# Four norms of a two-block network applied late: unscaled rows turned in halves inside neighbouring products

## The reference

```
# first block
h = rms_norm(x, norm_mix_g);  proj = h @ w_in            # 7 parts of 1024 columns
merged = sigmoid(g_a) * sgu(u, v) + sigmoid(g_b) * attention(q, k, v)
x = x + merged @ w_out
h = rms_norm(x, norm_ffn_g);  x = x + square(relu(h @ w_ff1)) @ w_ff2
gate = sigmoid(rms_norm(x, norm_ple_g) @ w_ple_gate);  x = x + gate * (p @ w_ple_proj)
x = rms_norm(x, norm_final_g)
# second block
h = rmsnorm(x, norm_mix);  z, xbc, dt, q, k, v = split(h @ w_in_2)
x = x + concat(ssd(conv(xbc), dt) gated by z, windowed attention(q, k, v)) @ w_out_2
h = rmsnorm(x, norm_ffn);  router: best group of 8, its 2 best of 8 experts
x = x + sum of gate * expert(h)                          # 64 experts, three matrices of 1024x512 each
out = rmsnorm(x, norm_final)
rms_norm(x, g) = x * rsqrt(mean(x * x) + 1e-6) * g
```

## Time and profile before

| | us |
|---|---|
| median of three runs | 1657.46 |
| lowest and highest | 1656.88 and 1661.55 |
| profiled execution, its own time | 1659.11 |
| its span, first to last instruction | 1657.3 |
| mean granted TensorE clock | 0.958 of full |
| busy in the span: PE / DVE / ACT / POOL | 1506.3 / 574.6 / 452.0 / 27.7 |

### The profile page before, as it was taken

One profiled execution on the slowest core, in us unless ns is written; L12 is line 12 of the kernel. 1 busy time (PEld: TensorE's weight loads), 2 busy tenths in 40 slices (PEclk: granted clock), 3 DMA queues, 4 the chain that ended last, 5 costly groups with the idle time before them and its releaser, 6 DMA issues.

```text
span 1657.3 us, 20152 instructions
## 1 busy us (share of the span) xinstructions
PE 1506.3 (91%) x7956; PEld 944.9 (57%) x7958; DVE 574.6 (35%) x926; ACT 452.0 (27%) x720; POOL 27.7 (2%) x36
## 2 busy tenths in 40 slices
PE   7999978999979987879999898889889889999996
PEld 5897868988759977763343343434334333444342
DVE  5745656654464897631111011111101101111112
ACT  5435645533444554421111011111101111111111
POOL 1000000000000000120000000000000000000000
PEclk9999989999989997979999999999999999999998
DMA  8563343455334332577999999999999999999993
GB/s 295 167 235 109 120 152 135 173 203 183 122 116 139 103 102 72 194 300 332 422 406 429 429 428 428 429 429 428 429 429 427 429 429 384 408 425 415 418 397 138
DMA packets 80269, 489.21 MB, mean 295 GB/s; under 512 B 6423, under 2 KB 8595, under 8 KB 56788
## 3 DMA queue, kind: packets, MB, share of 16 engines
q1 hardware_dynamic: 79028, 484.17, 72.4%
q0 software_dynamic: 1184, 4.26, 0.8%
HBM read 506.20 MB, written 1.08 MB: 306 GB/s over the span
## 4 chain that ended last, share of the span: by engine, by line
PE 61%; DMA 15%; DVE 8%; issue 2%; ACT 1%; SPq 1%; DVEq 0%; ACTq 0%
PE bank L1156 23%; PE bank L818 20%; DMA slots<-in_w_up_dram 15%; PE bank L1192 8%; PE bank L1126 4%; PE bank L1136 2%; DVE w_split L1292 1%; DVE h_lo L1282 1%; DVE areas L1542 1%; DVE xeT L1726 1%; PE bank L801 1%; SPq L394 1%; PE bank L1075 1%; PE bank L1104 0%; PE bank L1065 0%
## 5 line engine op out<-in xcount | busy, mean ns | idle before, releaser
L1156 PE MATMUL bank<-slots,xeT 128*64 128x512 f32 x1536 | 356.4, 620 | 48.0 <-DMA slots<-in_w_up_dram 47.9
L1156 PEld LDWEIGHTS bank<-slots,xeT 128*64 128x64 f32 x1536 | 118.9, 143 | 280.4 <-issue 280.4
L1292 DVE TENSOR_TENSOR w_split<-raw,w_split 128x2048 fp32r<-128x2048 f32 (+2 forms) x98 | 209.1, 2168 | 75.4 <-ACT w_split L543 75.4
L1192 PE MATMUL bank<-slots,heT 128*64 128x512 f32 x1024 | 226.8, 595 | 7.5 <-ACT heT L747 7.5
L818 PE MATMUL bank<-w_split,h_hi 128*128 128x512 f32 (+1 forms) x688 | 213.8, 393 | 8.4 <-DVE h_lo L1282 3.3
L818 PE MATMUL bank<-h_hi,w_split 128*128 128x256 f32 x1120 | 206.9, 285 | 0.3 <-DVE h_lo L1282 0.3
L543 ACT ACTIVATE w_split<-raw 128x2048 fp32r<-128x2048 f32 (+2 forms) x98 | 173.6, 1817 | 62.3 <-PE bank L818 56.7
L818 PEld LDWEIGHTS bank<-h_hi,w_split 128*128 128x128 f32 x1120 | 176.7, 193 | 2.2 <-issue 0.8
L1735 DVE TENSOR_TENSOR h_e<-bank,h_e 128x512 f32<-128x512 f32 x32 | 22.1, 692 | 433.2 <-PE bank L1156 433.2
L818 PE MATMUL bank<-h_lo,w_split 128*128 128x256 f32 x560 | 159.0, 284 | 0.0
L1192 PEld LDWEIGHTS bank<-slots,heT 128*64 128x64 f32 x1024 | 70.7, 137 | 144.9 <-issue 133.5
(11 more groups left out here) (295 smaller groups left out, 1390.5 us busy)
## 6 DMA issues: line engine op xcount, KB each, us to landing
slots<-in_w_up_dram SPq DMA_DIRECT2D x64, 2048.0 KB, 18.9
slots<-in_w_down_dram SPq DMA_DIRECT2D x64, 2048.0 KB, 15.2
areas<-in_w_gate_dram SPq DMA_DIRECT2D x32, 2048.0 KB, 14.2
slots<-in_w_gate_dram SPq DMA_DIRECT2D x32, 2048.0 KB, 21.3
raw<-in_w_in_dram SPq DMA_DIRECT2D x42, 1024.0 KB, 6.1
raw<-in_w_ff_dram SPq DMA_DIRECT2D x32, 1024.0 KB, 5.2
raw<-in_w_out_dram SPq DMA_DIRECT2D x12, 1024.0 KB, 5.0
raw<-in_w_ple_gate_dram SPq DMA_DIRECT2D x4, 1024.0 KB, 5.6
```

What stands on the lines that cost most here:

```text
L1156: last = mm(bank[SLOTS * e:SLOTS * e + SLOTS, :], xeT[:, k, odd, SLOTS * e:SLOTS * e + SLOTS], expert_panel(w, e, odd)[:, k, :], start=(k ...
L1192: last = mm(banks[half][SLOTS * e:SLOTS * e + SLOTS, :], heT[:, c, SLOTS * e:SLOTS * e + SLOTS], expert_panel("down", e, odd)[:, c, 512 * ...
L1292: last = tt(lo, source, hi, ALU.subtract)
```

## The change

At the four later norms x itself is turned, not a scaled copy. The first half of its columns (places 0 and 1 of `turn`, k tiles 0 to 3) is turned in the middle of the last product before the norm, into banks that are free (`turn_bank`), the second half behind that product. The factor 1/rms is computed from x beside the products and multiplied in later. For ff1 the square of it goes into the addition of the ff2 result. For pg it is the scale of the sigmoid. For the second block it goes into z and v (scale along rows), into the scores of the attention (rows), and by a row laid out along the tokens (`scale_row`, two matmuls against the identity) into k, dt and xbc, of which GpSimd scales the half that ScalarE empties. For the router it goes into the logits and into t_all. The panel pp moves before ff2 6, its product is kept in SBUF (p_proj), and GpSimd makes xg. norm_final_g comes a second time, as columns, by one more small load, so that the two gains are multiplied once.

```diff
-          + [("ff1", j) for j in range(8)] + [("ff2", j) for j in range(8)]
-          + [("pp", 0), ("pg", 0), ("pg", 1)]
+          + [("ff1", j) for j in range(8)] + [("ff2", j) for j in range(6)]
+          + [("pp", 0), ("ff2", 6), ("ff2", 7), ("pg", 0), ("pg", 1)]
...
+        def turn_bank(t, b):
+            if t in (T_FFN, T_MIX2):
+                return banks[pair_of(AT["wo" if t == T_FFN else "pg", b // 2]) + b % 2]
+            if t == T_PLE:
+                return banks[2 - pair_of(AT["pg", 0]) + b % 2]
+            return banks[b]
...
+                sp.dma_start(final_rows, norm_final_g.rearrange("(c p) -> c p", p=P)).then_inc(rows_loaded, 16)
```

GpSimd:

```diff
+            for half in range(2):
+                at = slice(512 * half, 512 * half + 512)
+                pool.wait_ge(x_ready, X_MLP + 2 * half + 2)
...
+                nc.gpsimd.tensor_tensor(xg[:, :, at], x[:, :, at], final_g[:, at].unsqueeze(1).to_broadcast([P, MT, 512]),
+                                        ALU.mult).then_inc(xg_ready, 1)
...
+            pool.wait_ge(row_ready, 1)
+            for j in range(3):
+                pool.wait_ge(emptied_a, emptied("a", AT["xbc", j]))
+                part = xraw[:, 4 * j:4 * j + 2, TAPS - 1:]
+                nc.gpsimd.tensor_tensor(part, part, scale_row.unsqueeze(1).to_broadcast([P, 2, S]), ALU.mult).then_inc(xbc_scaled, 1)
...
+            for half in range(2):
+                pool.wait_ge(x_ready, X_OUT1 + 2 * half + 2)
+                for m in range(MT):
...
+                    nc.gpsimd.tensor_tensor(to, row, gain, ALU.mult).then_inc(t_made, 1)
```

ScalarE, around ff1 and pg:

```diff
-            split_panel(AT["ff1", 0])
-            norm_x(T_FFN)
-            turn(T_FFN)
-            split_panel(AT["ff1", 1])
+            split(2 * AT["ff1", 0])
+            turn(T_FFN, (0, 1))
+            split(2 * AT["ff1", 0] + 1)
+            turn(T_FFN, (2, 3))
+            split(2 * AT["ff1", 1])
+            norm_x(emptied_d, emptied("d", AT["wo", 1]), xn)
+            split(2 * AT["ff1", 1] + 1)
...
+            for half in range(2):
+                for m in range(MT):
+                    act_(p_proj[:, m, 512 * half:512 * half + 512], banks[2 * half + m][:, :], ACT.Copy).then_inc(p_kept, 1)
+            split_panel(AT["ff2", 7])
+            split(2 * AT["pg", 0])
+            turn(T_PLE, (0, 1))
+            split(2 * AT["pg", 0] + 1)
+            turn(T_PLE, (2, 3))
+            split(2 * AT["pg", 1])
+            norm_x(x_ready, X_MLP, rows_area(3))
+            split(2 * AT["pg", 1] + 1)
```

ScalarE, the rows of h for the experts:

```diff
+            act.wait_ge(rstd_ready, norms[0])
+            for m in range(MT):
+                act.wait_ge(t_made, 3 + m)
+                link(act_(t_all[:, m, :], t_all[:, m, :], ACT.Copy, scale=stats[:, 8 + m:9 + m]))
                 act_(t_hi[:, m, :], t_all[:, m, :], ACT.Copy).then_inc(t_rounded, 1)
```

TensorE before ff1 (the other three joins are alike):

```diff
-            for j in range(2):
-                whole("wo", j, T_MERGED if j == 0 else None)
-
-            normed_turn(T_FFN, AT["wo", 1])
+            whole("wo", 0, T_MERGED)
+            quarter("wo", 1, 0)
+            quarter("wo", 1, 1)
+            banks_empty(AT["wo", 0])
+            turn(T_FFN, (0, 1))
+            quarter("wo", 1, 2)
+            quarter("wo", 1, 3)
+            hT_ready(T_FFN, 3)
+            part("ff1", 0, 0, (0, 1))
+            banks_empty(AT["wo", 1])
+            turn(T_FFN, (2, 3))
+            part("ff1", 0, 0, (2, 3))
+            hT_ready(T_FFN)
+            part("ff1", 0, 1, range(4))
```

TensorE in ff2 7, between its halves, and in pg 0:

```diff
+                    if j == 7 and k == 4:
+                        pe.wait_ge(p_kept, 4)
+                        pe.wait_ge(x_ready, 2)
+                        turn(T_PLE, (0, 1))
...
+            hT_ready(T_PLE, 3)
+            quarter("pg", 0, 0)
             pe.wait_ge(x_ready, X_MLP)
+            turn(T_PLE, (2, 3))
```

TensorE before q2: places 0 and 1 are turned after two quarters of pg 1, 2 and 3 after `part("q2", 0, 0, (0, 1))`; then the rest of q2 0, the product for dt, and:

```diff
+            pe.wait_ge(rstd_ready, 5)
+            for m in range(MT):
+                last = mm(banks[5][:, P * m:P * m + P], mix_scale[:, m:m + 1].to_broadcast([P, P]), ident[:, :], start=True, stop=True)
+            last.then_inc(row_made, 1)
```

TensorE before the router:

```diff
+            project_out(1, False, True, (0, 1))
+            pe.wait_ge(x_ready, X_OUT1 + 2)
+            turn(T_FFN2, (0, 1))
+            project_out(1, False, True, (2, 3))
...
+            route(0)
+            pe.wait_ge(x_ready, X_MIX2)
+            turn(T_FFN2, (2, 3))
+            route(1).then_inc(routed, 1)
```

VectorE, the ff2 result and the gate:

```diff
+                    stt(part, banks[4 + 2 * m + half][:, :], ffn_scale[:, m:m + 1], part, ALU.mult, ALU.add).then_inc(x_ready, 1)
...
+            def add_ple(half):
...
+                for m in range(MT):
+                    dve.wait_ge(emptied_a, emptied("a", AT["pg", half]) - 1 + m)
+                    link(tt(gate_rows[:, m, at], gate_rows[:, m, at], p_proj[:, m, at], ALU.mult))
+                    tt(x[:, m, at], x[:, m, at], gate_rows[:, m, at], ALU.add).then_inc(x_ready, 1)
...
+            add_ple(0)
+            split(2 * AT["q2", 0])
+            turn(T_MIX2, (0, 1))
+            split(2 * AT["q2", 0] + 1)
+            add_ple(1)
+            turn(T_MIX2, (2, 3))
+            split(2 * AT["q2", 1])
```

VectorE, second attention, convolution and router:

```diff
-                tt(soft[:, b, 0:S], bank[:, 0:S], mask, ALU.add)
+                    stt(soft[:, b, 0:S], bank[:, 0:S], mix_scale[:, 1:2], mask, ALU.mult, ALU.add)
+                    stt(soft[:, b, S:384], bank[:, S:384], mix_scale[:, 0:1], own, ALU.mult, ALU.add).then_inc(scores_taken, 1)
...
-                dve.wait_ge(emptied_a, emptied("a", AT["xbc", j]))
+                dve.wait_ge(xbc_scaled, j + 1)
...
+            for m in range(MT):
+                last = ts(logits[:, m, :], banks[m][:, 0:72], stats[:, 8 + m:9 + m], None, ALU.mult)
```

More of the change, by code:

```diff
@@ L724, in _ @@
             split_panel(AT["wo2", 1])
-            norm_x(T_FFN2)
-            turn(T_FFN2)
+            load_roots()
+            for half in range(2):
+                turn(T_FFN2, (2 * half + 1,))
+                for m in range(MT):
+                    part = slice(512 * half, 512 * half + 512)
+                    last = act_(rows_area(2)[:, m, part], x[:, m, part], ACT.Square,
+                                accum_out=stats[:, 2 * half + m:2 * half + m + 1])
+            last.then_inc(squares, 1)
+            norm(T_FFN2, MT)
+            act.wait_ge(rstd_ready, norms[0])
             for m in range(MT):
-                act.wait_ge(t_made, m + 1)
+                act.wait_ge(t_made, 3 + m)
+                link(act_(t_all[:, m, :], t_all[:, m, :], ACT.Copy, scale=stats[:, 8 + m:9 + m]))
                 act_(t_hi[:, m, :], t_all[:, m, :], ACT.Copy).then_inc(t_rounded, 1)
@@ L792, in banks_empty, with turn @@
                         pe.wait_ge(s, emptied(engine, p))
-            def turn(t):
+            def turn(t, places=range(4)):
                 src, _ = TURNS[t]
-                for b in range(4):
+                for b in places:
                     for k in (2 * b, 2 * b + 1):
@@ L856, in whole, with part @@
                     quarter(kind, j, c, fresh)
+            def part(kind, j, half, quarters):
+                p = AT[kind, j]
+                w, b0 = parts(p), pair_of(p)
+                pe.wait_ge(w_ready, 2 * p + half + 1)
+                for c in quarters:
+                    for k in range(4 * half, 4 * half + 4):
+                        last = product(banks[b0 + c // 2][:, S * (c % 2):S * (c % 2) + S], w, (every, k, slice(P * c, P * c + P)),
+                                       h, (every, k, every), c % 2 == 0 and k == 0, c % 2 == 1 and k == KT - 1, shared=True)
+                if half and quarters[-1] == 3:
+                    last.then_inc(panel_done, 1)
             def scores(n, q, k, k_tile):
@@ L1442, in _ @@
             empty("wo", 0)
[L1443 removed]
+            split(2 * AT["ff1", 0])
+            turn(T_FFN, (0, 1))
+            split(2 * AT["ff1", 0] + 1)
             empty("wo", 1)
[L1446 to L1448 removed]
+            turn(T_FFN, (2, 3))
+            split(2 * AT["ff1", 1])
+            dve.wait_ge(emptied_d, emptied("d", AT["wo", 1]))
+            sum_squares(x, D, xn)
+            rstd(MT, D)
+            link(tt(ffn_scale[:, :], stats[:, 8:10], stats[:, 8:10], ALU.mult))
+            split(2 * AT["ff1", 1] + 1)
             for j in range(8):
                 hidden(j, AT["ff1", j] + 2)
+            for j in (2, 3, 4):
+                split_panel(AT["ff2", j])
             dve.wait_ge(pT_rounded, 1)
@@ L1453, in _, with add_mlp @@
                 .then_inc(pT_ready, 1)
-            for p in range(AT["ff2", 2], AT["pg", 0]):
+            for p in (AT["ff2", 5], AT["pp", 0], AT["ff2", 6], AT["ff2", 7]):
                 split_panel(p)
-            dve.wait_ge(panel_done, AT["ff2", 7] + 1)
-            for b in range(4):
-                part = x[:, b // 2, 512 * (b % 2):512 * (b % 2) + 512]
-                tt(part, banks[4 + b][:, :], part, ALU.add).then_inc(x_ready, 1)
-            norm_x(T_PLE)
+            def add_mlp(half):
+                dve.wait_ge(panel_done, AT["ff2", 6 + half] + 1)
+                for m in range(MT):
```

(2 more changed lines are left out.)

287 lines of the change are left out of this document (150 added, 137 removed).

## The result

| | before | after |
|---|---|---|
| median of the comparison, us | 1657.17 (1656.54 to 1661.55) | 1632.07 (1629.25 to 1632.47) |
| profiled execution, its own time | 1659.11 | 1632.39 |
| its span | 1657.3 | 1630.2 |
| mean granted TensorE clock | 0.958 | 0.968 |

The ratio is 0.984, with a 95% interval of 0.982 to 0.986: 25.1 us faster by the medians, 26.7 by the two profiled executions. The forecast was 1633.7. Two later sets of executions of the same two kernels, taken with the experiments, give medians 23.3 and 25.7 apart.

A forecast was written before the change was run, and what follows sets the result against it. TensorE's products were taken to set the pace except at four norm joins and, in the second attention, VectorE; experts follow their first products. 4.7 + 5.5 + 12.4 + 5.4 - 3.7 - 0.5 = 23.8 us, forecast 1633.7, range 1626 to 1642.

The forecast's parts named there:

- Start: Kernel start: one more small load, one transpose and one small operation lose 0.5 us, bounds 0 to 1.
- Join 1: Norm before ff1: gap of 8.4 us less transposes 2.0 and a stall of 1.7, gain 4.7 us.
- Join 2: Norm before pg: 13.0 us less pp's warm products 5.5 and transposes 2.0, gain 5.5 us.
- Join 3: Norm before q2: 15.8 us less transposes 2.0, plus 1.4 for the cold clock, less new waits, gain 12.4 us.
- The stalls: Join 3: new waits of 1.1 us in pg 1, 0.7 after pg 1, 0.6 in the second q2 panel.
- The clock's share: Join 3: the cold clock goes, 120 products taking 14.4 us instead of 15.75, worth 1.4.
- Second attention: Scaled additions 1.3 us, k2 0.3, z 0.1 and GpSimd's xbc scaling 2.0 give a loss of 3.7.
- The hold-up: Second attention: GpSimd's in-place xbc scalings delay VectorE's two-input convolution steps, 2.0 us taken between 0 and 2.4.
- Join 4: Norm and routing before the experts: 18.6 us to the gather against 24.0, gain 5.4 us.
- rival A: VectorE never held up by GpSimd: 4.4 us in join 4 and 2.0 in the attention return, 1627.3; chance 0.22.
- other leg: Join 4: gained rows, ScalarE's four passes and GpSimd's second subtraction end at most 14.5 us after wo2's old end.
- Rivals B and C: B: three more stalls of about 2.5 us, 1641, chance 0.18. C: expert loads set the end, 1639, chance 0.08.

The follow-up runs named there:

- experiment 4: Changed kernel with the second half-panel of the second ff1 panel rounded ahead of the statistics; against the kernel before 0.983, median 1630.82 us.
- Experiment 1: Changed kernel with all 16 transposes behind the whole product in joins 1 to 3, no halves; against the kernel before 0.988, median 1639.84 us.
- experiments 5 and 6: Changed kernel without GpSimd's xbc scalings (5), or without the factor in the second attention's score additions (6); against the kernel before 0.962 and 0.997, other experts chosen.
- experiment 2: Changed kernel without GpSimd's two low-part subtractions, high part used twice in the first gathers; against the kernel before 0.982, median 1629.53 us.
- experiment 5: Changed kernel with GpSimd's three xbc scalings left out, then each with two more ahead of it; against the kernel before 0.962 (other experts chosen) and 0.987.
- first repeat: Changed kernel run again unchanged, as the measure beside experiments 5 and 6; against the kernel before 0.986, median 1634.31 us.
- two repeats: Changed kernel run twice more unchanged, as the measure beside later experiments; against the kernel before 0.986 and 0.985, medians 1634.31 and 1632.76 us.

## Why the prediction was right

**Start.** Loss 0.5 forecast, 0.6 measured.

**Join 1.** Gain 4.7 forecast, 4.5 + 0.6 = 5.1 measured. The stall in the second ff1 panel was put at 1.7 and came at 1.42, in the place and from the order of work named (statistics between the two half-panels); experiment 4 takes it away by changing that order alone.

**Join 2.** 5.5 forecast, 10.4 - 4.5 = 5.9 measured, without a stall.

**Join 3.** 12.4 forecast, 22.5 - 10.4 = 12.1 measured, in which the 0.3 for k2 is already lost (the wait before the first scores is 1.31, before it was 1.04). The stalls: 1.1 forecast and 0.71 measured, 0.7 and 0.69, 0.6 and 0.74. The clock's share comes out too: the forecast has 1.4 for it here, 1.8 in join 2 (7.29 against 5.5 for the products of pp), and counts the transposes of joins 1 and 3 at 1.97, which took 3.57 and 3.65 before, together 6.5; the trace has 5.6 less busy time over the three joins. Experiment 1 shows how much of these joins the halves are.

**Second attention.** 3.7 forecast, 0.3 + 2.7 = 3.0 measured. From head 5 to head 15 the kernel before took 611.3 - 553.6 = 57.7, the changed one 60.3. Of these 2.6, experiments 5 and 6 show 1.6 (2.0 forecast) and 1.1 (1.3 forecast for 11 heads). The hold-up was mis-sized by a little: each scaling takes 1.09, and 0.78 of it falls on a waiting operation (2.31 - 1.53).

**Join 4.** 5.4 forecast, 25.8 - 19.8 = 6.0 measured. Its main uncertain term, VectorE held up by GpSimd's subtractions, was taken as 4.4 between 0 and 4.8. The two operations of 2.01 and 2.33 hold 1.70 + 2.02 = 3.7, and experiment 2 gets 3.7 back; so rival A is out. A third, not foreseen, is the sum of the two halves of the squares: two columns in 0.72 at 701.81, beside GpSimd's gained rows (698.47 to 702.51). No run took it apart. With it the hold-up comes to 4.3, next to the 4.4 taken, but 0.55 of that lies in a place that the prediction didn't name. Its sum for this join has small slips that change nothing: the terms up to the end of the router add up to 6.7 (6.9 stands there), and by its own other leg free running would give 24.0 - 14.5 = 9.5 (9.3 stands there) and rival A 4.1 instead of 4.4. The Trainium skill (SBUF — State Buffer, "SBUF: two separate sides") names the condition that experiment 5 ran into, two SBUF inputs against a GpSimd operation that reads SBUF; the trace agrees, with 0.30 for the one-input reduction at 705.77 and 2.01 for the two-input comparison at 706.11, both under the same subtraction.

**Rivals B and C.** No stall came in another place than those named: TensorE is not idle in front of ff2 7 or pg 0, and in q2 0 only for the 0.69 that was forecast as 0.7. The gather came 25.8 earlier and the end 27.1, and the DMA engines still rest before the experts, so the expert stage did move with its first products. The gather comes 18.0 us after the end of wo2 (18.6 forecast), if wo2 is taken to end 24.6 us after T_SSD is turned from, as in the trace before.

**What the sum lacks.** Up to the gather the terms give 23.8 and the trace 25.8; joins 1, 2 and 4 gave 0.4 to 0.6 more each, the attention lost 0.7 less. Of the end's further 1.3 I had no term. From the first expert product to the end it took 910.9 before and 909.6 after, but in the other runs with the changed kernel's loads 907.4 to 910.4, so 1.3 is less than what executions differ by. The medians lie 25.1, 23.3 and 25.7 apart in three sets, about the 23.8 of the sum. The forecast of 1633.7 came within 1.6 of the median 1632.07 partly by luck: it took 1.65 off the profiled execution's time, as in the three executions before, while in the changed kernel median and profiled execution are 0.3 apart; for the profiled execution 1635.3 was forecast and 1632.39 measured.

## What to carry to other kernels

A row factor of a norm can leave the path if the rows are used in products: use them unscaled, and multiply where results leave the banks; here that gave 16 us in three joins (a moved product included, and 5.5 of them as less busy time at a higher clock), and turning half the columns inside the product before gave 7 more. Statistics that nobody waits for must not stand ahead of a weight split that somebody waits for, since in-order engines turn them into a stall (1.4 and 0.7 here). In these runs work handed to GpSimd was only free where VectorE had no operation with two SBUF inputs beside it, or did not set the end; beside a chain of small VectorE operations, two subtractions on GpSimd cost 3.7 us, and 2.5 us on VectorE itself behind the chain cost 0.2 (from the router to the first expert product 20.24 us, against 718.76 - 698.70 = 20.06 without any low parts).

## What the runs showed of the hardware

The hold-up goes both ways. In join 3 of the changed kernel GpSimd waits for VectorE's weight split, and takes 4.38 where the same operation takes 2.39 with no VectorE operation of two SBUF inputs beside it (timeline of DVE and POOL):

```profile
457.54 2.28 DVE L1384 TENSOR_TENSOR w_split<-raw,w_split 128x2048 fp32r<-128x2048 f32 x1
457.71 4.38 POOL L481 TENSOR_TENSOR areas<-x,areas 128x1024 f32<-128x1024 f32 x1 [233.23 <-DVE x L1596]
...
467.82 2.39 POOL L481 TENSOR_TENSOR areas<-x,areas 128x1024 f32<-128x1024 f32 x1 [5.73 <-DVE x L1596]
```

Executions differ by lumps of 1.6 to 2.0 us. Two of them could be traced to TensorE's products running at about half speed for longer. One lies behind the wait of 1.3 for dt. Two executions of the same program (windows; the columns as in the earlier trace rows), first the one shown throughout, then the first repeat:

```profile
506.00:513.00 7.00, 7.00 (x39) 6.47 (x40) 4.39 (x18) 4.40 (x9) 0.00 (x0) 0.76 0.01 2
```

```profile
507.40:514.40 7.00, 6.96 (x29) 6.38 (x29) 3.72 (x16) 4.40 (x9) 0.00 (x0) 0.51 0.01 4
```

The granted clock averages 0.76 of full in the one, between its two levels of 1.2 and 2.4 GHz, and 0.51, nearly all at the lower, in the other: 39 instructions of TensorE against 29 in 7 us. The second head's scores come 1.6 after the first's in the one (510.7, 512.3) and 3.2 in the other (512.1, 515.3). Another lump lies at the very first products: in the two repeats they run 0.43 apart instead of 0.23, up to 19.4 us in the one and 19.8 in the other, though the granted clock of that stretch reads 1.00 in all three. What decides it, no run here shows.
